# A weight transfer of 128 rows sent as eight transfers of 8 rows and one of 64 rows

## The reference, cut to what matters

```
for e in range(32):                                   # all 32 experts
    hu = t @ w_gu[e] + b_gu[e]                        # w_gu[e]: 1024 x 2048
    glu = minimum(hu[:, :1024], 7.0)
    lin = clip(hu[:, 1024:], -7.0, 7.0)
    act = glu * sigmoid(1.702 * glu) * (lin + 1.0)
    y = y + gates[:, e:e+1] * (act @ w_dn[e] + b_dn[e])   # w_dn[e]: 1024 x 1024
```

## Time and profile before

| what | value |
|---|---|
| time, median of 3 runs | 1129.52 us (1129.49 to 1129.54) |
| the profiled execution's own time | 1129.2 us |
| its span, first to last instruction | 1127.4 us |
| TensorE matmuls busy | 1069.5 us, 95% of the span |
| SP's queue (q1) | 41824 packets, 431.07 MB, 91.3% of 16 DMA engines' span |
| chain that ended last | PE 70%, DMA 26% |

### The profile page before, as it was taken

How to read it: one execution, slowest core, us unless ns; L and a number is a source line. 1 busy time by engine, 2 the same in 40 slices (tenths; PEclk the granted TensorE clock), 3 DMA queues, 4 the chain that set the end, 5 groups by cost and what they waited for, 6 DMA issues and landing times.

```text
span 1127.4 us, 11952 instructions
## 1 busy us (share of the span) xinstructions
PE 1069.5 (95%) x5102; PEld 447.9 (40%) x5102; DVE 255.4 (23%) x529; ACT 145.1 (13%) x281; POOL 16.7 (1%) x40
## 2 busy tenths in 40 slices
PE   6999999999999999999999999898989999999988
PEld 3476554434343434343434333333333344434234
DVE  2364333221212121212121112121211021212122
ACT  3234433000000000000000000000000100000021
POOL 2000200000000000000000000000000000000000
PEclk9999999999999999999999999999999999999999
DMA  9942549999999999999999999999999999999971
GB/s 348 335 173 81 213 161 420 428 427 429 427 426 427 426 428 427 429 427 427 427 428 427 427 428 428 427 427 427 428 428 426 427 428 428 428 426 427 427 304 38
DMA packets 41950, 431.89 MB, mean 383 GB/s; under 512 B 5944, under 2 KB 6464, under 8 KB 17064
## 3 DMA queue, kind: packets, MB, share of 16 engines
q1 hardware_dynamic: 41824, 431.07, 91.3%
q10 hardware_dynamic: 72, 0.04, 0.0%
HBM read 430.04 MB, written 1.06 MB: 382 GB/s over the span
## 4 chain that ended last, share of the span: by engine, by line
PE 70%; DMA 26%; ACT 2%; issue 1%; DVE 1%; ACTq 0%; DVEq 0%
PE hu L957 26%; DMA ring<-in_w_gate_up 22%; PE po L985 14%; PE aux L916 5%; PE hu L624 5%; DMA ring<-in_w_down 4%; PE aux L924 3%; PE hu L630 3%; PE hu L639 2%; PE hu L949 2%; PE aux L1142 1%; PE po L964 1%; ACT early L1739 1%; PE hu L985 1%; PE po L1142 1%
## 5 line engine op out<-in xcount | busy, mean ns | idle before, releaser
L957 PE MATMUL hu<-ring,num_xg 128*64 128x512 f32 x1920 | 432.8, 596 | 14.3 <-DMA ring<-in_w_gate_up 14.3
L957 PEld LDWEIGHTS hu<-ring,num_xg 128*64 128x64 f32 x1920 | 134.1, 137 | 292.4 <-issue 258.6
L985 PE MATMUL po<-ring,early 128*64 128x512 f32 x992 | 220.8, 595 | 25.3 <-ACT early L1739 11.8
L985 PEld LDWEIGHTS po<-ring,early 128*64 128x64 f32 x992 | 74.2, 137 | 151.7 <-issue 136.4
L1457 DVE TENSOR_SCALAR early<-hu 128x512 f32<-128x512 f32 x32 | 22.1, 692 | 442.3 <-PE hu L957 442.3
L1443 DVE TENSOR_TENSOR xt<-xt,aux 128x512 f32<-128x512 f32 x66 | 42.4, 684 | 161.7 <-PE aux L924 142.1
L624 PE MATMUL hu<-ring 128*128 128x512 f32 x144 | 63.8, 596 | 0.0
L916 PEld LDWEIGHTS aux<-early,big 128*128 128x128 f32 x512 | 58.4, 192 | 13.0 <-issue 13.0
L924 PE MATMUL aux<-num_xg,early 64*128 64x512 f32 x248 | 61.9, 616 | 0.7 <-ACT num_xg L1743 0.7
L916 PE MATMUL aux<-early,big 128*128 128x128 f32 x512 | 61.4, 278 | 0.0
L1735 ACT ACTIVATE hu<-early 128x512 f32<-128x512 f32 x32 | 19.2, 601 | 259.9 <-DVE early L1457 259.9
(11 more groups left out here) (241 smaller groups left out, 539.5 us busy)
## 6 DMA issues: line engine op xcount, KB each, us to landing
ring<-in_w_gate_up SPq DMA_DIRECT2D x128, 2048.0 KB, 35.7
ring<-in_w_down SPq DMA_DIRECT2D x62, 2048.0 KB, 37.2
ring<-in_w_in SPq DMA_DIRECT2D x7, 2048.0 KB, 15.1
ring<-in_w_out SPq DMA_DIRECT2D x2, 2048.0 KB, 8.1
ring<-in_w_ple_gate SPq DMA_DIRECT2D x2, 2048.0 KB, 37.5
ring<-in_w_down SPq DMA_DIRECT2D x3, 1024.0 KB, 10.7
xt<-in_x SPq DMA_DIRECT2D x2, 512.0 KB, 4.2
ring<-negm_scratch SPq DMA_DIRECT2D x1, 1024.0 KB, 7.0
```

What stands on the lines that cost most here:

```text
L957: last = mm(hu[n * SLOTS:(n + 1) * SLOTS, 2 * e + b, :], rows_of[:, k, e * SLOTS:(e + 1) * SLOTS], w[:, o:o + NB], start=(k == 0), stop=(k ...
L985: last = mm(bank[n * SLOTS:(n + 1) * SLOTS, :], actT[:, f, h * SLOTS:(h + 1) * SLOTS], w[:, o:o + NB], start=(h == 0 and f == 0), stop=(h ...
```

## The change

Position 170 is issued as nine transfers: eight of 8 rows (partitions 0 to 63, in order) and one of 64 rows (partitions 64 to 127). The eight add to a new semaphore, `groups_loaded`, and the one of 64 rows adds to the slot's own semaphore. TensorE waits for both before the chunk's first matmul. Rows, bytes, addresses and the order among positions are as before.

```diff
+    ROW_GROUPS_AT = 170
+    ROW_GROUP = 8
...
+    assert AT[ROW_GROUPS_AT][1] == 0
...
+        groups_loaded = sem("groups_loaded")
...
                 if m in HALVED:
                     sp.dma_start(dst[:, 0:2 * D], src[:, 0:2 * D]).then_inc(half_loaded, 16)
+                elif m == ROW_GROUPS_AT:
+                    for r in range(0, P // 2, ROW_GROUP):
+                        sp.dma_start(dst[r:r + ROW_GROUP, :], src[r:r + ROW_GROUP, :]).then_inc(groups_loaded, 16)
+                    sp.dma_start(dst[P // 2:P, :], src[P // 2:P, :]).then_inc(full, 16)
                 else:
                     sp.dma_start(dst, src).then_inc(full, 16)
...
                         if m in HALVED:
                             wait_half(pe, ps, m)
+                        elif m == ROW_GROUPS_AT:
+                            groups = P // 2 // ROW_GROUP
+                            pe.wait_ge(groups_loaded, ps * (16 * groups) + 16 * groups)
                         wait_position(pe, ps, m)
```

## The result

| | before | after |
|---|---|---|
| median | 1129.51 us (1129.22 to 1129.54, 4 runs) | 1142.39 us (1141.39 to 1144.54, 4 runs) |
| profiled execution, its span | 1129.2, 1127.4 us | 1141.39, 1139.6 us |
| ratio | | 1.0115, 95% interval 1.0102 to 1.0127 |

The change costs 12.9 us, where 4.7 were forecast. It is slower, as said, and inside the range, but 2.7 times as much, and within the figures of rival A (+8.8 to +14.5). The profiled execution is the fastest of the four; it and its span are 12.2 us longer than before.

A forecast was written before the change was run, and what follows sets the result against it. The prediction took SP's full transfer queue to bound the kernel. From 1129.2 us it added 8.8 of slip less 4.1 of lead, +4.7, giving 1133.9, or 1134.2 us as median; the 8-in-10 range was 1128.3 to 1143.5.

The forecast's parts named there:

- rival A: At position 170, lagging DMA engines or a mix get the small transfers, no lead covers the slip: +8.8 to +14.5, chance 0.25.
- What bounds the kernel: SP's full transfer queue sets the end until 1076.4 us, so delaying its last transfers delays the end one for one.
- Part 1: At position 170, eight DMA engines, always the same, get 12 rows and the others 4: 2.45 us later and earlier.
- Part 2: Eight neighbouring partitions take in 53 GB/s, 2.47 us per transfer in step; staggered, the eight small transfers take 10 us.
- The 64-row part lies on the other 64 partitions: The 12-row group's 4 rows of position 170's 64-row transfer take 3.7 us, between 2.45 alone and 4.9 at half rate.
- Part 3: Eight DMA engines run 4 to 8 us ahead at the stream's end; their lead hides 4.1 us of the slip.
- If the small transfers go to the leading eight: The forecast's assumed case at position 170: the stream ends 4.7 us later (+2.5 to +8), chance 0.50.
- 8.8 of slip: The 12-row group leaves position 170 later by 8.8 us: 13.7 us in place of 4.9.
- Part 4: SP's nine issues take 3 to 5 us but cost nothing, nor does TensorE's extra wait before position 170 (at most 0.1 us).
- B: DMA engines keep in step at position 170, each 8-row transfer taking 2.47 us: +15.7, 1145.2 us, chance 0.05.
- C: Small transfers at position 170 stagger perfectly on the leading eight, the lead hides their slip: faster, 1127.9 us, chance 0.12.
- D: Each 8-row transfer uses another eight DMA engines, position 170's 4.0 us slack hides the rest: within 1 us of 1129.5, chance 0.08.

The follow-up runs named there:

- the kernels with one side spread: The change with its small transfers writing partitions 4 apart but reading neighbouring rows, 1138.31 us; or reading rows 4 apart but writing neighbouring partitions, 1142.62 us.
- the two halves: Against the kernel before, position 170 issued as two transfers of 64 rows, partitions 0 to 63 and 64 to 127: 1139.29 us.
- position 3: The same nine-transfer split made at position 3 in place of 170, into an empty queue: 1129.21 us.
- position 26: Two kernels split position 26 in place of 170: as two transfers of 64 rows, 1136.78 us; as the change's nine transfers, 1144.9 us.
- the kernel with sixteen: Against the changed kernel, position 170 issued as sixteen transfers of 8 rows, each on partitions 4 apart, with no 64-row transfer: 1143.9 us.

## Why the prediction missed the size

**What bounds the kernel**: right. The slip of position 170 went through a full queue to the end, 12.2 us of 13.6, and the waits of the last pair kept their size.

**Part 1, which DMA engines**: right in the count. 12 rows against 4 cost nearly what it says (1.6 to 2.3 us of 2.4), and 16 rows on the eight 4.6 of 4.9.

**Part 2, how fast 8 rows go in**: the place was right, and the kernels with one side spread show that it is the partitions written. The scaling from 32 partitions to 8 gave 2.47 us; in lockstep it measured 1.9. At position 170, where the DMA engines are staggered, the rows were faster than that (0.93 to 1.84 us from 970 to 980), as I had argued. What was wrong is whom it slows, and this is the first of two steps that failed. I let only the eight be slow and gave the others "full rate". The runs show the whole stream at 206 to 269 GB/s for as long as any DMA engine is in the narrow place, those with ordinary rows too. "The 64-row part lies on the other 64 partitions", at 3.7 us, was mis-sized likewise: two such parts alone cost 10.0 us. The prediction had no term for the rows of the others, and put their slowing at nothing without a reason.

**Part 3, the lead**: the other step that failed. "If the small transfers go to the leading eight" was a coin that I called at 0.50, and it came down mixed. By the completion times two of the eight were lagging ones. So the 4.1 us that I subtracted covered next to nothing. The kernel with 8 rows on the eight and none elsewhere would have ended earlier if all lagging ones had been outside; it ended where it was. Even a won toss would not have given the 4.1 us: the flow that is lost is lost on the lagging DMA engines too, as the two halves show, with 8 rows on each and +10.0, so a lead could have hidden the 2.4 us of extra rows at most. And a lead doesn't only hide. The two halves cost +7.4 at a spread of 1.8 us and +10.0 at 6.7. I put that down to the leading ones, which bring the slowness in while the others are still on the transfer before; the windows of position 170 show this, that it is the whole difference they don't.

The two errors pull the same way: 8.8 of slip should have been 13.4 (11.0 of lost flow and 2.4 of rows), and 4.1 of lead should have been none. That makes 13.4, measured are 12.9, against 4.7.

**Part 4**: right. Nine issues took 3.3 us of SP, and no row shows anyone waiting for them. The sum has no term for TensorE's granted clock. It did fall to 0.50 in the wait of 7.1 us, and no cost of that shows at the end.

**The rivals**: A had the number (+8.8 to +14.5) and its reason, "a mix of both groups", but not the slowing of the rest. B, lockstep at position 170, didn't occur there; it did at position 3, and nearly at 26. C and D are out. The Trainium skill's "SBUF — State Buffer", section on the DMA port swizzle, was the right guide to the place: by its map the halves reach 8 ports of 16, the even partitions all 16, and these cost 10.0 and 0 us.

What stays open: why all 16 are slowed. The traces show that they are, at positions 3, 26 and 170, and that the side written starts it. Where between the DMA engines and the partitions the queue forms, none of these runs tells, nor why transfers of 8 rows 4 apart are free on partitions 0 to 63 and not on 64 to 127.

## What to carry to other kernels

If a transfer in a full queue has to be split, split it so that each piece still spreads over all 128 partitions (by even and odd rows, not by halves or blocks): in this kernel two pieces cost nothing that way, and 10 us as halves. When the queue is the bound, cost a narrow transfer by what the whole stream loses while it is in flight, not by its own bytes. And don't count on a lead of some DMA engines before you know which of them get the work.

## What the runs showed of the hardware that I had not expected

Rows onto 8 neighbouring partitions slow down transfers that write elsewhere, to the same pace: 1.95 us a row for all 16 DMA engines at position 3, 134 GB/s in all. In the changed kernel, all but a few of the rows that start at one moment take about the same time (0.62 us at 965.2, 0.97 at 965.9, 1.25 at 987), though at 965.9 and at 987 some write to position 170's narrow place and others don't.

On partitions 0 to 63, 8-row transfers on partitions 4 apart are as cheap per byte as one of 128 rows (426 GB/s with eight of them in the stream), even behind and ahead of full transfers; on 64 to 127, in the kernel with sixteen, the stream ran at half rate. The count of transfers and completions doesn't show in any time here: nine in place of one cost -0.6 us in the kernel without the 64-row part.

The DMA engines of one queue drift apart: one transfer's 16 completions are 1.8 us apart at 260 us, 6.7 at position 170 and 8.0 at the end. The price of what is sent changes with it: the same two halves cost 7.4 us early and 10.0 us late, and the same small transfers 15.0 early and 12.9 late. That the spread is the cause is argued from the windows; position 26 and position 170 differ in more than that.
